# First norm by pairs of scale and shift blocks, with the first pw1 block's products in step with its rows

## The reference, cut to what matters

```python
mod = jax.nn.silu(c) @ p['w_mod'][i] + p['b_mod'][i]
sh1, sc1, g1, sh2, sc2, g2 = jnp.split(mod, 6, axis=-1)
h = modulate(rms_norm(x, p['norm_mix'][i]), sh1, sc1)      # h * (1 + sc1) + sh1
# conv_module(h, ...):
a, gt = jnp.split(h @ w_pw1 + b_pw1, 2, axis=-1)
u = a * jax.nn.sigmoid(gt)
up = jnp.concatenate([state, u], axis=1)
z = depthwise_conv(up, w_dw, width 31) + b_dw
z = jax.nn.silu(layer_norm(z, ln_g, ln_b))
y = z @ w_pw2 + b_pw2
x = x + g1 * y
```

## Time and profile before

| | |
|---|---|
| runs shown (us) | 3746.40, 3705.44, 3302.58; median 3705.44 |
| profiled execution | 3301.68 us; span of its slowest core (5) 3300.6 us, other cores from 3281.4 us |
| busy, share of the span | TensorE 92%, its weight loads 56%, VectorE 37%, ScalarE 22%, POOL 9% |
| TensorE clock granted, mean | 0.956 of full speed on core 5 |
| chain that ended last | TensorE 82%, DMA 6%, VectorE 5%, ScalarE 3%, issue 3% |
| head: first pw1 product | 155.98 us from the span's start |
| conv stage | about 156 to 530 us |

### The profile page before, as it was taken

The page is one execution under the profiler, slowest core; times in us unless marked ns, Lnnn a source line. Parts: engine busy times, 40 slices in busy tenths (PEclk is TensorE's granted clock), DMA queues, the critical chain, the costliest instruction groups (busy, mean ns, idle before and its releaser), DMA issues.

```text
span 3300.6 us, 58445 instructions; the slowest of 8 cores (3281.4 to 3300.6 us)
## 1 busy us (share of the span) xinstructions
PE 3030.2 (92%) x23566; PEld 1862.0 (56%) x23566; DVE 1234.4 (37%) x2763; ACT 738.3 (22%) x1710; POOL 290.2 (9%) x474
## 2 busy tenths in 40 slices
PE   2399997879999999999999989898999999999997
PEld 0155554445556565565565555455666666666664
DVE  0356766442321413113412647733231222223416
ACT  1412225551000000000002547655100000000013
POOL 0000000000000000000001025410000000000000
PEclk8599998989999999999999999789999999999999
DMA  9877764625756476573667122133584435443442
GB/s 221 152 114 127 131 116 104 132 39 100 131 96 131 75 135 115 99 137 72 116 119 131 30 53 49 30 63 60 101 137 70 77 66 84 69 77 56 86 77 106
DMA packets 73592, 320.57 MB, mean 97 GB/s; under 512 B 11952, under 2 KB 28176, under 8 KB 45808
## 3 DMA queue, kind: packets, MB, share of 16 engines
q0 software_dynamic: 49440, 283.78, 49.2%
q1 hardware_dynamic: 23888, 33.06, 3.5%
HBM read 590.55 MB, written 10.70 MB: 182 GB/s over the span
## 4 chain that ended last, share of the span: by engine, by line
PE 82%; DMA 6%; DVE 5%; ACT 3%; issue 3%; another core or an unknown queue 1%; SPq 0%; DVEq 0%; ACTq 0%; POOL 0%; POOLq 0%
PE ps L230 81%; DMA RING<-wmod 2%; ACT SCR L233 2%; DMA X<-xT 1%; DMA RING<-wgu 1%; DMA RING<-wpw 1%; PE ps L1394 1%; ACT RING L233 1%; DVE SCR L544 1%; ACT HBraw L233 1%; DVE UBraw L1400 0%; DVE X L457 0%; SPq L225 0%; DVE X L952 0%
## 5 line engine op out<-in xcount | busy, mean ns | idle before, releaser
L230 PE MATMUL ps<-HBraw,RING 128*128 128x384 bf16 (+4 forms) x10848 | 1767.0, 325 | 39.1 <-ACT SCR L233 21.2
L230 PEld LDWEIGHTS ps<-HBraw,RING 128*128 128x128 bf16 x10848 | 1051.7, 98 | 722.6 <-issue 58.3
L230 PE MATMUL ps<-UBraw,RING 128*128 128x384 bf16 (+3 forms) x6016 | 964.8, 319 | 29.5 <-ACT UBraw L233 19.8
L230 PEld LDWEIGHTS ps<-UBraw,RING 128*128 128x128 bf16 x6016 | 572.4, 99 | 395.7 <-issue 65.3
L627 DVE TENSOR_TENSOR UBraw<-ps,SCR 128x384 bf16<-128x384 f32 (+2 forms) x264 | 144.3, 547 | 1190.7 <-PE ps L230 1171.2
L233 ACT ACTIVATE SCR<-ps 128x384 f32<-128x384 f32 (+2 forms) x264 | 127.1, 482 | 1772.2 <-PE ps L230 1772.1
L466 DVE SCALAR_TENSOR_TENSOR X<-ps,MOD,X 128x384 f32<-128x384 f32 (+2 forms) x960 | 388.8, 446 | 290.5 <-PE ps L230 289.1
L230 PE MATMUL ps<-SCT,RING 128*128 128x3 bf16 x3072 | 91.4, 165 | 61.8 <-DMA RING<-wmod 52.0
L225 POOL DMA_DIRECT2D RING<-wgu x88 | 46.6, 529 | 1073.0 <-PE ps L230 1069.7
L225 POOL DMA_DIRECT2D RING<-wmod x96 | 52.0, 542 | 941.4 <-PE ps L230 932.6
L230 PEld LDWEIGHTS ps<-SCT,RING 128*128 128x128 bf16 x3072 | 89.8, 97 | 72.2 <-issue 64.4
(11 more groups left out here) (96 smaller groups left out, 1213.3 us busy)
## 6 DMA issues: line engine op xcount, KB each, us to landing
RING<-wmod POOLq DMA_DIRECT2D x96, 1024.0 KB, 12.4
RING<-wgu POOLq DMA_DIRECT2D x88, 1024.0 KB, 9.2
RING<-wdn POOLq DMA_DIRECT2D x80, 512.0 KB, 8.9
RING<-wpw POOLq DMA_DIRECT2D x24, 1024.0 KB, 16.5
X<-xT SPq DMA_DIRECT2D x4, 2368.0 KB, 54.6
RING<-wqkv POOLq DMA_DIRECT2D x16, 512.0 KB, 6.5
X<-xT SPq DMA_DIRECT2D x32, 192.0 KB, 2.6
RING<-wo POOLq DMA_DIRECT2D x5, 1024.0 KB, 9.5
```

The lines of the kernel that those rows point to most:

```text
L230: return PE.emit(nc.tensor.matmul(out, lhsT=lhsT, rhs=rhs, start=start, stop=stop, **kw))
```

## The change

The order of the loads and of the products changes in layer 0's first norm and in pw1; no operation on the data is left out.
- Plan: scale and shift blocks alternate (8, 0, 9, 1, ...), in the zone of halves 0 to 5, three blocks. pw1_0 comes behind block 3 and has halves 6 to 8 to itself. pw1_1 still lies in the small zone; from mod0_16 on the zone is the whole ring. The blocks 16 to 31 come one chunk later each, and mod0_31 last.
- During the quarters of x two mod_blocks run per quarter (8+q and q). The pair loop makes AM for two chunks at a time, and takes blocks 12 and 4 in its second round, and 8+b and b for b of 5 and more.
- ScalarE scales the odd chunk of a pair first. Chunk 14 is scaled by VectorE.
- `pw1_first(c)` multiplies one row of HB with all six parts of pw1_0 into the banks 0, 1, 4 and 2, 3, 5; these stay open over all rows. Rows 0 to 5 are queued in round 3, then two a round, and 15 and 14 last. `pw1_chunk(0)` only does the sigmoid and GLU part, now in `pw1_rows`.
- After the loop over c, mod_block(0, 31) runs in bank 7.

```diff
@@ -261,15 +261,20 @@
             plan.append((name + "b", 8, src[:, 8:16, :], zone[0]))
 
 
-        for b in (*range(8, 16), *range(7)):
+        for b in range(8):
+            zone[0] = (0, 6)
+            wblock(f"mod0_{8 + b}", wmod[8 + b], KC)
             wblock(f"mod0_{b}", wmod[b], KC)
-        for c in range(16):
+            if b == 3:
+                zone[0] = (6, NHALF)
+                wblock("pw1_0", wpw1[0], KC)
+        for c in range(1, 16):
             wblock(f"pw1_{c}", wpw1[c], KC)
-            if c == 0:
-                wblock("mod0_7", wmod[7], KC)
-            wblock(f"mod0_{16 + c}", wmod[16 + c], KC)
+            zone[0] = (0, NHALF)
+            wblock(f"mod0_{15 + c}", wmod[15 + c], KC)
             if c % 2 == 1:
                 wblock(f"mod0_{32 + c // 2}", wmod[32 + c // 2], KC)
+        wblock("mod0_31", wmod[31], KC)
         for b in range(8):
             wblock(f"pw2_{b}", wpw2[b], KC)
         for li in range(2):
@@ -690,10 +695,12 @@
             yield
 
 
+
         tiles1 = [(0, 512), (512, 1024), (1024, NH)]
         sq_free = [None, None]
         for q in range(4):
-            mod_block(0, 8 + q, 4 + q % 2)
+            mod_block(0, 8 + q, 0)
+            mod_block(0, q, 7)
             for c in range(4 * q, 4 * q + 4):
                 ACT.wait(t_x0[q], sq_free[c % 2])
                 act(SQ[:, c % 2, 32:NH], X[:, c, :], AF.Square)
@@ -709,34 +716,62 @@
         ACT.wait(PE.tick())
         for bank, lo, a, b_ in ((PS[6], 0, 0, 32), (PS[1], 32, 32, 512), (PS[2], 0, 512, 1024), (PS[3], 0, 1024, NH)):
             act(RSTD[:, a:b_], bank[:, lo:lo + b_ - a], AF.Ln, bias=EPSC[:, 0:1], scale=1.0 / D)
-        ACT.wait(ACT.tick())
+        bfree[1] = bfree[2] = bfree[3] = bfree[6] = ACT.tick()
+        ACT.wait(bfree[6])
         act(RSTD[:], RSTD[:], AF.Exp, scale=-0.5)
         t_rstd = ACT.tick()
-        for b in range(12, 16):
-            mod_block(0, b, 4 + b % 2)
-        DVE.wait(DVE.tick())
-        DVE.emit(nc.vector.scalar_tensor_tensor(out=AM[:], in0=MOD[:, 0, 16:32, :], scalar=1.0,
-                                                in1=VTs[:, VO["nmix"]:VO["nmix"] + 16].unsqueeze(2).to_broadcast([128, 16, 3]),
-                                                op0=ALU.add, op1=ALU.mult))
         DVE.wait(t_rstd)
         t1_free = [None, None]
         hb0_t = {}
-        first = None
+        first = first_bi = None
+
+        def pw1_first(c):
+            PE.wait(hb0_t[c])
+            for half in range(2):
+                for i, (a, b_) in enumerate(tiles1):
+                    bk = (0, 1, 4)[i] if half == 0 else (2, 3, 5)[i]
+                    if c == 0:
+                        PE.wait(bfree[bk])
+                    mm(PS[bk][:, 0:b_ - a], first[:, c, 128 * half:128 * half + 128], HB[:, c, a:b_], c == 0, c == KC - 2)
+
         for b in range(8):
             for c in (2 * b, 2 * b + 1):
                 Tc = (T1, T1B)[c % 2]
                 DVE.wait(t1_free[c % 2])
                 DVE.emit(nc.vector.tensor_tensor(out=Tc[:, 0:32], in0=XP[:, c, :], in1=RSTD[:, 0:32], op=ALU.mult))
                 DVE.emit(nc.vector.tensor_tensor(out=Tc[:, 32:NH], in0=X[:, c, :], in1=RSTD[:, 32:NH], op=ALU.mult))
-            if b == 7:
-                first = ring_use("pw1_0")
-            mod_block(0, b, 4 + b % 2)
-            ACT.wait(DVE.tick())
-            for c in (2 * b, 2 * b + 1):
+            if b == 1:
+                first, first_bi = ring_use("pw1_0")
+            if b >= 5:
+                mod_block(0, 8 + b, 6)
+                mod_block(0, b, 7)
+            DVE.wait(DVE.tick())
+            DVE.emit(nc.vector.scalar_tensor_tensor(out=AM[:, 2 * b:2 * b + 2, :], in0=MOD[:, 0, 16 + 2 * b:18 + 2 * b, :], scalar=1.0,
+                                                    in1=VTs[:, VO["nmix"] + 2 * b:VO["nmix"] + 2 * b + 2].unsqueeze(2).to_broadcast([128, 2, 3]),
+                                                    op0=ALU.add, op1=ALU.mult))
+            t_am = DVE.tick()
+            ACT.wait(t_am)
+            for c in (2 * b + 1, 2 * b):
                 Tc = (T1, T1B)[c % 2]
                 for a, b_, bi in ((0, 1184, 0), (1184, 1200, 1), (1200, 1216, 2)):
-                    act(HB[:, c, a:b_], Tc[:, a:b_], AF.Identity, scale=AM[:, c, bi:bi + 1], bias=MOD[:, 0, c, bi:bi + 1])
-                t1_free[c % 2] = hb0_t[c] = ACT.tick()
+                    am, sh = AM[:, c, bi:bi + 1], MOD[:, 0, c, bi:bi + 1]
+                    if c == KC - 2:
+                        DVE.wait(t_am)
+                        DVE.emit(nc.vector.tensor_scalar(out=HB[:, c, a:b_], in0=Tc[:, a:b_], scalar1=am, scalar2=sh,
+                                                         op0=ALU.mult, op1=ALU.add))
+                    else:
+                        act(HB[:, c, a:b_], Tc[:, a:b_], AF.Identity, scale=am, bias=sh)
+                t1_free[c % 2] = hb0_t[c] = DVE.tick() if c == KC - 2 else ACT.tick()
+            if b == 1:
+                mod_block(0, 12, 6)
+                mod_block(0, 4, 7)
+            if b >= 3:
+                for c in range(0 if b == 3 else 2 * b - 2, 2 * b):
+                    pw1_first(c)
+        for c in (KC - 1, KC - 2):
+            pw1_first(c)
+        t_first = PE.tick()
+        ring_release(first_bi)
 
 
         DVE.wait(t_st, t_wp)
@@ -747,7 +782,7 @@
         gfree = [None, None]
         sgfree = [None, None]
         uf_t = [None, None]
-        cfree = [None, None, None]
+        cfree = [None, None, bfree[6]]
         sqfree = [None, None]
         u4_t = {}
         u4a_t = []
@@ -755,49 +790,60 @@
         ncv = 0
         kk = 0
 
+        def pw1_rows(c, a, b_, ba, bgt, tpa, tpg, i):
+
+            cb, ncols = c % 2, b_ - a
+            ACT.wait(tpg, sgfree[i])
+            act(SGC[:, i, 0:ncols], bgt[:, 0:ncols], AF.Sigmoid, bias=VTs[:, VO["bpg"] + c:VO["bpg"] + c + 1])
+            t_sig = ACT.tick()
+            DVE.wait(t_sig, tpa)
+            ba_s = VTs[:, VO["bpa"] + c:VO["bpa"] + c + 1]
+
+            def glu(out, lo, hi):
+                DVE.emit(nc.vector.scalar_tensor_tensor(out=out, in0=ba[:, lo:hi], scalar=ba_s,
+                                                        in1=SGC[:, i, lo:hi], op0=ALU.add, op1=ALU.mult))
+            if a < 1024:
+                glu(U[:, cb, a:b_], 0, ncols)
+                if a == 512 and c == KC - 1:
+                    late_shift(c)
+            else:
+                glu(U[:, cb, 1024:1184], 0, 160)
+                glu(U[:, cb, 1214:1230], 160, 176)
+                glu(U[:, cb, 1260:1276], 176, 192)
+                DVE.wait(uf_t[cb])
+                glu(UFs[:, cb, 0:30], 130, 160)
+                glu(UFs[:, cb, 30:62], 160, 192)
+            t_u = sgfree[i] = DVE.tick()
+            if a == 0:
+                DVE.wait(t_u)
+                DVE.emit(nc.vector.tensor_scalar_mul(out=U[:, cb, 0:160], in0=U[:, cb, 0:160], scalar1=FLAG[:, 0:1]))
+            if b_ == NH:
+                SP.wait(t_u)
+                uf_t[cb] = dma(SP, ucT[128 * c:128 * c + 128, :], UFs[:, cb, :], uf_sem[cb])
+            return t_u, t_sig
+
         def pw1_chunk(c):
             nonlocal kk
-            cb = c % 2
-            slot, bi = ring_use(f"pw1_{c}") if c > 0 else first
+            if c == 0:
+                for i, (a, b_) in enumerate(tiles1):
+                    t_u, t_sig = pw1_rows(0, a, b_, PS[(0, 1, 4)[i]], PS[(2, 3, 5)[i]], t_first, t_first, i % 2)
+                    if i < 2:
+                        afree[i], gfree[i] = t_u, t_sig
+                    else:
+                        cfree[0] = cfree[1] = t_u
+                return
+            slot, bi = ring_use(f"pw1_{c}")
             for (a, b_) in tiles1:
-                ncols = b_ - a
-                ba, bgt = PS[kk % 2], PS[2 + kk % 2]
-                PE.wait(afree[kk % 2], gfree[kk % 2])
+                ncols, i = b_ - a, kk % 2
+                ba, bgt = PS[i], PS[2 + i]
+                PE.wait(afree[i], gfree[i])
                 for k in range(KC):
-                    PE.wait(hb0_t[k])
                     mm(ba[:, 0:ncols], slot[:, k, 0:128], HB[:, k, a:b_], k == 0, k == KC - 1)
                 tpa = PE.tick()
                 for k in range(KC):
                     mm(bgt[:, 0:ncols], slot[:, k, 128:256], HB[:, k, a:b_], k == 0, k == KC - 1)
...
+                afree[i], gfree[i] = pw1_rows(c, a, b_, ba, bgt, tpa, PE.tick(), i)
                 kk += 1
-            SP.wait(afree[(kk - 1) % 2])
-            uf_t[cb] = dma(SP, ucT[128 * c:128 * c + 128, :], UFs[:, cb, :], uf_sem[cb])
             ring_release(bi)
 
         def shift_copies(c, lo, hi, both=False):
@@ -879,7 +925,8 @@
 
         for c in range(KC):
             pw1_chunk(c)
-            mod_block(0, 16 + c)
+            if c > 0:
+                mod_block(0, 15 + c)
             shift_chunk(c)
             if c > 0:
                 conv_chunk(c - 1)
@@ -889,6 +936,7 @@
```

(29 more changed lines are left out.)

## The result

The kernel became slower by a little, where I had forecast no change: the ratio to the kernel before is **1.0059, interval 1.0043 to 1.0075**, 19.5 us on 3302.58. The profiled execution took 3317.94 us (forecast 3302).

What follows compares the result with a forecast made beforehand. TensorE, busy 92% of the span, was taken to bound the kernel, with the head waiting on loads. Head -3.8, pw1_2's wait -0.6 and tail +4.5 summed to +0.1: 3302 us, range 3287 to 3320.

Steps and rivals of the forecast that it cites:

- Part 1: When RSTD is ready: x's last quarter lands at 94.3 instead of 86.20, RSTD at 105.4 us, 8.1 us late.
- my share: In the load stage, x keeps 0.25 of its lone progress while weight blocks are in flight, 8 us a block.
- The starved rival: In the loads, x gets 0.125; last quarter at 114.8, RSTD at 125.9, +20.5 us, 3322 us; chance 0.18.
- the second rival of the list: In the loads, queues take even turns, 0.5 for x; RSTD at 100.5 us, 3297 us in all; chance 0.15.
- T: Time when RSTD is ready in layer 0's first norm, from which later steps are counted; forecast 105.4 us.
- Part 2: Pair loop: with ScalarE taking the odd row first, VectorE waits; 7.25 us a pair, unhindered some 5.6.
- Part 3: pw1_0 in step with the rows: rows 0 to 5 from T+21.6, mod0_7 at T+55.3, pw1_0 complete at T+62.3.
- Part 4: Hand-over to pw1_1: TensorE waits 3.05 us for sigmoid and GLU; pw1_1 starts at 170.8, 3.8 us gained.
- Part 5: End of the conv stage: mod0_31 waits for VectorE's eviction of mod0_39; conv 15 starts 4.5 us later, taken whole.
- The rival out of step: In the head, TensorE does rows 0 to 7 after the last load, costing the 3.05 hand-over; about 3309 us; chance 0.03.
- The sum: Whole kernel: -3.8 - 0.6 + 4.5 = +0.1, giving 3302 us.

Runs made afterwards that it cites:

- holding the weights: Changed kernel, with POOL waiting for x's last quarter before it issues pw1_0 and the blocks behind it; 1.0019 of the kernel before.
- the end undone: Changed kernel, with mod0_31 taken in chunk 14 as before; 1.0061 of the kernel before.
- the even row first: Changed kernel, with ScalarE scaling the even row of each pair first, as before, except in the last pair; 1.0066 of the kernel before.
- the places undone: Changed kernel, with gu0_16 moved in the ring so that kv_v replaces dn0_5_3 and dn0_5_4, used up early; 1.0037 of the kernel before.
- out of step: Changed kernel, with all 96 products of pw1_0 behind mod0_7 in TensorE's queue; 1.0085 of the kernel before.
- the two experiments on it: gu0_21 moved in the kernel before, giving kv_v the changed kernel's halves: 1.0037; gu0_16 moved in the changed kernel, giving kv_v early-freed halves: 1.0037.

## Why the prediction was wrong

**Part 1 failed in its size.** "x's last 3.8 take 15.2 us: 94.3 instead of 86.20." The kind is shown by holding the weights (13 us), and my share was about right: 204 and 211 GB/s in the windows above give (204-166)/164 = 0.23 and 0.27. But two terms of the count were off. The second quarter came earlier than I had it (59.7 to 64.4, not 67.3), so mod0_3 and pw1_0 went out at 67 to 71 instead of 74.3, and x was hardly ever alone: by the windows of core 1 above, from 80 us to its last quarter, 8 x 0.23 + 8 x 0.27 + 8 x 0.23 + 5.6 x 0.09 gives 6.3 us of x left at 80, where I had 3.6. (The last term takes the share of a window that runs on past the quarter; up to 109.63 alone it was 187 GB/s, and the sum 6.6.) And the loads of mod0_12, mod0_4 and mod0_13 hang on the third quarter's squares. Core 4, with at least as much left (8 x 0.29 + 7.2 x 0.58 = 6.5, and rather more, since its engines were busy for only 0.79 of the second window), had its third quarter later and its last quarter sooner. Its ScalarE, its POOL and two windows:

```profile
87.60 2.27 ACT L233 ACTIVATE SCR<-X 128x1184 bf16<-128x1184 f32 x2 [23.05 <-DMA X<-xT]
...
95.17 2.27 ACT L233 ACTIVATE SCR<-X 128x1184 bf16<-128x1184 f32 x2 [2.73 <-DMA X<-xT]
```

```profile
94.58 0.53 POOL L225 DMA_DIRECT2D RING<-wmod  x1 [26.57 <-PE ps L230]
95.39 1.05 POOL L225 DMA_DIRECT2D RING<-wmod  x2 [0.28 <-issue]
```

```profile
80.00:88.00 8.00, 0.00 (x0) 0.00 (x0) 0.00 (x0) 0.40 (x1) 0.00 (x0) 0.50 0.99 214
88.00:96.00 8.00, 5.34 (x75) 2.82 (x76) 0.69 (x4) 4.96 (x5) 1.14 (x3) 0.71 0.79 262
```

Core 1 had issued the same three at 86.66 and 87.51, ahead of x's rest. In the table the five cores with the third quarter by 82.3 have the last one from 100.6 on, and the three with it from 87 on have it by 97.2. A third quarter that lands early lets three more weight blocks in front of the last: the cores differ by up to 10.5 us in the third quarter and, the other way round, by up to 14.4 in the last. The four other kernels that leave this part alone (the end undone, the even row first, the places undone, out of step) show the same: third quarter by 81.3 us, last at 99.0 to 110.5 (14 cores); third from 84.0 on, last at 94.6 to 99.6 (10 cores). I had counted one core, and with one outcome. What makes the third quarter land at 79 on one core and 88 on another was not tried.

The rule on turns that stood beside part 1 (the Trainium skill, DMA: Bandwidth & Descriptors, Queues, rings and completion order: each engine takes the queues that have work in turn) does not give even shares here: x got 0.20 to 0.29 with blocks queued (windows of 198 to 214 GB/s, cores 1 and 4 of the kernel after), and 0.22 to 0.28 before. No run shows how large the packets of the two queues are. (Even turns are the second rival of the list, not the third.)

**The starved rival** (3322 us, chance 0.18) came nearest: it had the last quarter at 114.8 and T at 125.9, against 109.6 and 122.0 on the slowest core. It was right in result for half the reason: the share wasn't halved, the loads were earlier. That its 3322 us is the measured 3302.58 and 19.5 is luck, since it knew nothing of the second loss. Its 20.5 us for the head are 16.4 on core 1 (pw1_1 at 173.80 before, 190.16 after).

**Part 2** was right: 7.17 us a pair, and the order within the pair is its cause.

**Part 3** was right in the ring's order and nearly in its times. (ScalarE's end of pair 6 comes out of its own 7.25 us a pair as T+50.6, not T+52.1; it was T+51.1, and nothing hung on it. Part 1 had a like slip: 67.3 + 5.5 + 1 is 73.8, not 74.3, which would have put the last quarter 1.5 us later.) Rows 0 to 5 were no burst at T+21.6: only mod0_12 and mod0_4, which are in, stand ahead of them in TensorE's queue on the chip, so they ran two by two from pair 0 on, up to 4.21 us a pair at the half clock that I had allowed for. That changes nothing behind them, since mod0_13 still waits for the row of pair 3, and came at T+32.7 as worked out. mod0_7 was 1.7 later than forecast, and the rows behind it took 7.9 us to 186.9 instead of 7.0.

**Part 4**: the hand-over was 3.25 us (forecast 3.05, with "3 us of idle TensorE"). The start of pw1_1 wasn't earlier, since T had moved by 27.3 on this core (94.70 before).
"All later products of the stage stand in the same order" is **the sentence that failed by what it left out**. It holds for the products and their queues; the loads keep their order too, but not their places. I never followed the ring past the stage, where the measured wait for kv_v is 9.1 to 11.4 us at about 1856 us, and costs some 8 us.

**Part 5** was right in place and nearly in local size: 5.8 us of wait, conv 15 begins 4.5 us later behind mod0_39 (7.66 against 3.16, core 5, after and end undone), and of these 3.9 reach the first pw2 product. As a share of the whole it is not shown apart from zero: 0.11% when put in, nothing when taken out.

**The rival out of step**: 3309 against 3302 was the step's worth, 7 us; measured 8.6 in this kernel (1 to 16), 7 by the head alone.

**The sum.** The forecast's own account was +0.1. Measured, of 19.5 us: about 13 for x behind the weights, about 7 to 9 for kv_v's place, and the rest, the end of the stage among it, within what the intervals leave. The split is rough. Between the slowest cores of the two profiled executions (5 before, 1 after) 15.6 of the 16.2 us lie ahead of the first pw2 product; behind it core 1 has 10.1 us of wait for kv_v and is still only 0.6 us longer, so the rest of its way must have been shorter by as much; where was not followed. What kv_v's place costs is read from the two experiments on it, not from this pair.

## What to carry to other kernels

When a change frees ring slots earlier, ask first what transfer the new loads will overtake: activations that everything waits for lose to queued weights, and the loss differs by core (last quarter at 95.2 to 109.6 us here), and the slowest core sets the time. When blocks are placed behind one another in a ring, a block added, dropped or moved can change the neighbours of nearly all later ones (the new start did here, moving mod0_31 did not): list the places at each stage's border before and after, and look for the load that has come to stand on the last-used block. Load what everything waits for alone and first; work under the loads pays in full only once the loads never stop (11 us against 7 here, by the start of pw1_1).
